# A hybrid decoder layer on one core: block stores from two queues, the block load ahead of the decay row, SiLU in the third chunk, the inverse at later places

## What is computed

```python
q, k, v = split(silu(short_conv(concat([q, k, v]), conv_w)))     # q, k then made unit length
a_mat = where(strict, (k * beta) @ k.T * decay, 0)               # per head and chunk
t_mat = triangular_solve(eye + a_mat, eye)                       # the inverse
u, w = t_mat @ (v * beta), t_mat @ (k * beta * exp(g))
v_new = u - w @ s                                                # s: the running state
o = (q * exp(g)) @ s + (q @ k.T * decay) @ v_new
s = s * exp(g_last) + k_dec.T @ v_new
y = layer_norm(alpha * x + concat([rms_norm(o) * norm_w * silu(z_a), swa * silu(z_b)]) @ w_out)
```

## Time and profile before

| | |
|---|---|
| time, median of 3 runs | 1247.62 us (1246.43 to 1248.07) |
| profiled execution: its own time | 1249.48 us |
| profiled execution: span from the first to the last instruction | 1247.7 us |
| busy: PE, PEld, DVE, ACT, POOL | 1149.6, 900.9, 650.1, 505.5, 198.0 us |
| mean granted clock of TensorE | 0.970 |

### The profile page before, as it was taken

The page is one execution under the profiler, slowest core; times in us unless marked ns, Lnnn a source line. Parts: engine busy times, 40 slices in busy tenths (PEclk is TensorE's granted clock), DMA queues, the critical chain, the costliest instruction groups (busy, mean ns, idle before and its releaser), DMA issues. The chain is left out here.

```text
span 1247.7 us, 19748 instructions
## 1 busy us (share of the span) xinstructions
PE 1149.6 (92%) x7340; PEld 900.9 (72%) x7340; DVE 650.1 (52%) x1996; ACT 505.5 (41%) x1475; POOL 198.0 (16%) x268
## 2 busy tenths in 40 slices
PE   4988989888999999999999999999899989899997
PEld 2766767666777868786786878777686868687776
DVE  3345554645355464646356364745437363636565
ACT  3363636363352625353352433336233534353220
POOL 4522323122210101023000101012100000000340
PEclk9998989898999999999999999999999999999999
DMA  6753745545572543632436362625244343522232
GB/s 212 287 191 123 252 164 161 179 136 153 161 237 102 164 160 104 211 127 78 150 132 193 124 192 79 201 84 172 85 165 157 110 137 110 168 79 61 94 109 84
DMA packets 63887, 183.57 MB, mean 147 GB/s; under 512 B 16240, under 2 KB 28976, under 8 KB 50480
## 3 DMA queue, kind: packets, MB, share of 16 engines
q1 hardware_dynamic: 63792, 182.32, 44.1%
HBM read 138.22 MB, written 44.07 MB: 146 GB/s over the span
## 5 line engine op out<-in xcount | busy, mean ns | idle before, releaser
L760 PE MATMUL bank<-xr,w 128*128 128x512 f32 x2496 | 684.8, 414 | 5.1 <-ACT conv_in L1091 3.2
L760 PEld LDWEIGHTS bank<-xr,w 128*128 128x128 f32 x2496 | 455.5, 193 | 108.5 <-issue 14.8
L733 POOL TENSOR_TENSOR x_tile<-x_tile,gain 128x256 f32<-128x256 f32 x40 | 28.1, 736 | 716.6 <-DVE x_tile L1484 716.6
L810 PE MATMUL bank<-wo,y_split 128*128 128x512 f32 x432 | 118.8, 409 | 0.0
L810 PEld LDWEIGHTS bank<-wo,y_split 128*128 128x128 f32 x432 | 76.2, 188 | 17.1 <-issue 1.9
L1410 DVE SCALAR_TENSOR_TENSOR kq<-conv_in,convw_all,kq 128x512 f32<-128x512 f32 x96 | 76.5, 796 | 3.4
L1332 ACT ACTIVATE blocks<-bank 128x128 f32<-128x128 f32 x64 | 17.8, 277 | 149.0 <-PE bank L1027 148.8
L1605 DVE TENSOR_TENSOR y_step<-blocks,y_cols 128x60 f32<-128x60 f32 (+14 forms) x240 | 49.7, 207 | 49.7 <-DMA blocks<-n_spill 42.0
L1227 ACT ACTIVATE score<-score,neg_max 128x256 f32<-128x256 f32 (+1 forms) x128 | 62.5, 490 | 16.8 <-DVE neg_max L1572 16.8
L1297 ACT ACTIVATE blocks<-bank 128x256 f32<-128x256 f32 (+1 forms) x64 | 24.4, 382 | 105.1 <-PE bank L974 73.7
L1692 DVE SCALAR_TENSOR_TENSOR t<-bank,cols_all,v_tok 128x128 f32<-128x128 f32 x64 | 22.3, 348 | 84.8 <-PE bank L1012 84.8
(11 more groups left out here) (214 smaller groups left out, 1762.1 us busy)
## 6 DMA issues: line engine op xcount, KB each, us to landing
w<-w_split SPq DMA_DIRECT2D x78, 1024.0 KB, 5.0
w_split<-w SPq DMA_DIRECT2D x26, 1024.0 KB, 4.9
blocks<-n_spill SPq DMA_DIRECT2D x16, 512.0 KB
y_spill<-y_out SPq DMA_DIRECT2D x30, 256.0 KB, 6.3
y_tile<-w_in SPq DMA_DIRECT2D x13, 512.0 KB, 6.1
x_tile<-w_in SPq DMA_DIRECT2D x13, 512.0 KB, 6.2
y_tile<-y_spill SPq DMA_DIRECT2D x12, 512.0 KB, 6.7
x_tile<-x SPq DMA_DIRECT2D x12, 512.0 KB, 5.6
```

The costliest lines, as they stand in the source:

```text
L733: nc.gpsimd.tensor_tensor(res[:, part], res[:, part], gain[:, part], ALU.mult).then_inc(scaled.sem, 1)
L760: ins = nc.tensor.matmul(bank[at % 2][:], w[:, turn % 3, wp, k, :], xr[:, xp, k], start=(step == 0), stop=(step == 3 * KT - 1))
L810: ins = nc.tensor.matmul(bank[at % 2][:], y_place(t)[:, yp, k], wo[:, k, wp, half * UNIT:(half + 1) * UNIT], start=(step == 0), stop=(step ...
```

## The change

1. `store_blocks` on SyncE's queue issues five of the eight block stores; ScalarE issues the other three, behind the squares of q and ahead of the scaled k, with a wait for `n_ready`.
2. `load_blocks` stands right behind the block stores; the decay row, the input loads of long slots, weights and the spill come behind it.
3. `AT_VTOK` goes from 0.13 to 0.16. In `Places`, `first` (the place of t0, from which the inverse's places count) goes from 0.47, 0.42, 0.36 (short, middle, long) to 0.49, 0.44, 0.375, `step0` and `step` from 0.665 and 0.082, 0.62 and 0.092, 0.6 and 0.097 to 0.685 and 0.077, 0.635 and 0.088, 0.605 and 0.096.
4. The SiLU stands ahead of the third chunk's squares where the jobs that it needs end early enough, which is so in short and middle slots, and ahead of the fourth's as before in long ones. In middle slots the job bz changes places with o1. The split of the next y tile on VectorE moves from the third to the fourth chunk.
5. The exponential of the decay row (`eg_row`) stands ahead of the squares of k.
6. Where a slot's last job is followed by a `w_hi` (slots 0 and 1), that is held until behind the block stores of the next slot.

```diff
--- before.py
+++ after.py
@@ -39,6 +39,7 @@
 BASE = 16
 HALF = P // 2
 PIECES = 4
+SP_BLOCKS = 5
 TILES_W = 26
 TAIL = 12
 
@@ -62,7 +63,7 @@
     if i == AH - 1:
         return ["z"] + (["o0", "o1"] if s > 0 else []) + unit_start
     if s == 1 or s == 2:
-        return ["q", "k", "v", "z", "o0", "o1", "bz", "bq"]
+        return ["q", "k", "v", "z", "o0", "bz", "o1", "bq"]
     return ["q", "k", "v", "bz", "z", "bq"]
 
 
@@ -154,7 +155,7 @@
 
 
 AT_KK = 0.04
-AT_SCORES0, AT_VTOK, AT_TURNS0, AT_VALUES0 = 0.09, 0.13, 0.24, 0.31
+AT_SCORES0, AT_VTOK, AT_TURNS0, AT_VALUES0 = 0.09, 0.16, 0.24, 0.31
 
 
 class Places:
@@ -163,9 +164,9 @@
     def __init__(self, n):
         fill = slot_span(n)
         short, long = fill < 160, fill > 200
-        first = 0.47 if short else 0.36 if long else 0.42
+        first = 0.49 if short else 0.375 if long else 0.44
         self.t0, self.p16, self.t16, self.p32, self.t32, self.p64, self.y12 = (first + 0.028 * a for a in range(7))
-        self.step0, self.step = (0.665, 0.082) if short else (0.6, 0.097) if long else (0.62, 0.092)
+        self.step0, self.step = (0.685, 0.077) if short else (0.605, 0.096) if long else (0.635, 0.088)
         self.scores1 = self.p16 + 0.015
         self.turns1, self.values1 = self.step0, self.step0 + 0.05
         self.base = 0.3
@@ -585,7 +586,7 @@
 
             def store_blocks(n):
                 after(sp, n_ready, n, CH)
-                for g in range(P // BASE):
+                for g in range(SP_BLOCKS):
                     part = slice(g * BASE, (g + 1) * BASE)
                     sp.dma_start(n_spill[n, g].rearrange("t a c -> a t c"), n_t[part, :, part]).then_inc(n_stored.sem, 16)
 
@@ -634,13 +635,13 @@
                     for dst, source in ((gain, ln_g), (shift, ln_b)):
                         sp.dma_start(dst[:], source).then_inc(gain_in, 16)
                 store_blocks(n)
+                load_blocks(n)
                 if i < AH - 1:
                     after(sp, pt_ready, n, 2)
                     load_decay(n + 1)
                 if i == AH - 1 and 0 < s < SBS - 1:
                     after(sp, x_low_dve, s + 1, 1)
                     load_x(s + 1, 3)
-                load_blocks(n)
                 after_jobs(n, 0.16)
                 if n > 0:
                     spill_a(n - 1)
@@ -1108,6 +1109,12 @@
                 nc.scalar.activation(own[:, EKD], own[:, EKD], ACT.Exp).then_inc(cols_ready.sem, 1)
 
             place = [0]
+            held = []
+
+            def split_weight():
+
+                while held:
+                    w_hi(held.pop())
 
             def after_job(at):
                 job = JOBS[at]
@@ -1144,7 +1151,10 @@
                 elif kind == "gT":
                     copy(g_turned, at, gt_copied)
                 if at in W_AT and W_AT[at] + 3 < TILES_W:
-                    w_hi(W_AT[at] + 3)
+                    if at + 1 < len(JOBS) and JOBS[at + 1].n > max(job.n, -1) >= 0:
+                        held.append(W_AT[at] + 3)
+                    else:
+                        w_hi(W_AT[at] + 3)
                 k = {"ba": 0, "q": 1, "k": 2, "v": 3, "kb": 4, "vb": 5, "bz": 6, "bq": 7}.get(kind)
                 if n == AH - 1 and k is not None:
                     wo_hi(k)
@@ -1242,6 +1252,9 @@
             def slot(n):
                 s, i = divmod(n, AH)
                 at = Places(n)
+                after(act, g_row_in, n, 16)
+                after(act, resid_ready, n - 1, CH)
+                nc.scalar.activation(eg_row[:], decay[:], ACT.Exp).then_inc(eg_ready.sem, 1)
                 after(act, ktok_done, n, 1)
                 for c in range(CH):
                     nc.scalar.activation(n_t[:, c], bank[4][:, c * P:(c + 1) * P], ACT.Square,
@@ -1250,9 +1263,6 @@
                 nc.scalar.activation(ln_ss[:, 0], sums_sq[:, 0], ACT.Ln, bias=eps[:, 0:1]).then_inc(ln_ready.sem, 1)
                 after(act, ln_ready, n, 1)
                 nc.scalar.activation(r_k[:], ln_ss[:, 0], ACT.Exp, scale=-0.5).then_inc(rk_ready.sem, 1)
-                after(act, g_row_in, n, 16)
-                after(act, resid_ready, n - 1, CH)
-                nc.scalar.activation(eg_row[:], decay[:], ACT.Exp).then_inc(eg_ready.sem, 1)
                 if i == 0:
                     after(act, vt_done, s, 1)
                     first = 4 * s % 8
@@ -1264,6 +1274,11 @@
                 for c in range(CH):
                     nc.scalar.activation(k_dec[:, c], bank[5][:, c * P:(c + 1) * P], ACT.Square,
                                          accum_out=sums_sq[:, 1, c:c + 1]).then_inc(sq_done.sem, 1)
+                after(act, n_ready, n, CH)
+                for g in range(SP_BLOCKS, P // BASE):
+                    part = slice(g * BASE, (g + 1) * BASE)
+                    act.dma_start(n_spill[n, g].rearrange("t a c -> a t c"), n_t[part, :, part]).then_inc(n_stored.sem, 16)
+                split_weight()
                 after(act, small, n, 3)
                 after(act, sq_done, n, 2 * CH)
                 for c in range(CH):
@@ -1314,11 +1329,16 @@
                 take(p64[high], half_tiles(bank[6])[high], 8)
                 after_jobs(n, at.y12)
                 take(y_inv[low, :, high], half_tiles(bank[7])[low], 9)
-                after_jobs(n, at.step0)
+                after_jobs(n, min(at.step0, 0.66))
                 copy_turned(n, 1)
+                silu_before = CH - 2 if silu_at(n) - n < at.chunk(CH - 2) and n < SLOTS - 1 else CH - 1
                 for c in range(CH):
+                    if c == silu_before:
+                        after_jobs(n, max(at.chunk(c), silu_at(n) - n))
+                        if c < CH - 1:
+                            silu(n, True)
                     if c == CH - 1:
-                        after_jobs(n, max(at.chunk(c), silu_at(n) - n))
+                        after_jobs(n, at.chunk(c))
                         if t is not None and i == AH - 2:
                             round_y(t + 1)
                         elif n == SLOTS - 2:
@@ -1326,7 +1346,8 @@
                         if n == SLOTS - 1:
                             round_y(14)
                             round_y(15)
-                        silu(n, True)
+                        if silu_before == c:
+                            silu(n, True)
                     after_jobs(n, at.chunk(c, 2 / 3))
                     after(act, o_done, n, c + 1)
                     nc.scalar.activation(o_scaled[:, c], bank[7][:, c * P:(c + 1) * P], ACT.Square,
@@ -1705,7 +1726,7 @@
                         convs(n, (at.p64, at.chunk(0), 1)[c])
                     if n == SLOTS - 1 and c < 3:
                         split_y(11 + c)
-                    if c == 2:
+                    if c == CH - 1:
                         if t is not None and i == AH - 2:
                             split_y(t + 1)
                         elif n == SLOTS - 2:
```

## The result

The changed kernel is slower. Its median is 1256.6 us (ten runs, 1252.5 to 1263.8) against 1247.8 us for the kernel before (ten runs, 1246.4 to 1250.8); the ratio is 1.0070, 95% interval 1.0049 to 1.0092. I had forecast 1222 us. The profiled execution of the changed kernel took 1253.1 us and is one of the low ones; its span is 1251.1 us against 1247.7, so the traces show 3.4 us of the some 9.

What follows compares the result with a forecast made beforehand. TensorE, busy 1149.6 of 1247.7 us, bounds the kernel; only its idling or low clock can be won. Savings 20.4 + 5.7 + 1.8 - 0.2 - 3.3 - 10.9 + 11.9 = 25.4 us gave 1222, range 1204 to 1243.

Steps and rivals of the forecast that it cites:

- bz ahead of o1: Middle slots: VectorE normalises last, SyncE is held until 7 us into the next slot; about 4.5 us lost.
- In slots 6 and 10 L953 at 12 covers that: The transposes, 12 us into these slots, release the block load anyway, so the held SyncE queue costs nothing there.
- A landing 2 us later in slots 5 and 9: Some 2.5 MB pass ahead of the block load; t0 waits 1.9 and 2.6 us instead of 1.0 each.
- The weights behind the held queue: A weight load behind SyncE's held output store; TensorE waiting for weights was a sign of being wrong, without a size.
- In 7 and 11 the x tile comes 1.0 too late: Behind held SyncE, the x tile is 1.0 us late for VectorE and L881 in each slot, 2.0 together.
- the transposes' place: Moved 0.03 of a slot later, 1.2 to 1.5 us; block load 0.5 later in slot 10, against 0.9 gained.
- t0, all slots: TensorE's waits for the base inverse at t0 in 16 slots fall from 44.8 to 24.4 us, saving 20.4.
- third chunk's squares, L1019: New TensorE wait behind the moved SiLU: 1.5 us in slots 2 and 12 to 14, 2.45 in 0 and 1; 10.9.
- clock, busy time saved: TensorE's low-clock losses behind waits fall from 14 to 7, at 1.7 us each; 11.9 us saved.
- The rival of the near waits: Twelve remaining TensorE waits between 1.37 and 2.4 us also lower the clock; 20.4 more, 1242 us; chance 0.20.
- the slower rival: ScalarE's DMA issues cost 1.8 us each, scaled k comes 5.5 behind N, TensorE waits at L948; 1261 us; chance 0.08.
- The earlier N: Moved SiLU and exponential bring N 1.85 us earlier in slots 13, 14, 3 and 15, 3.1 in 1 and 2.

Runs made afterwards that it cites:

- swap_back: Changed kernel with o1 ahead of bz again in the six middle slots; 1236.7 us, ratio 0.9936 to the kernel before.
- norm_early: Changed kernel, bz still ahead of o1, middle slots' output tiles normalised 0.05 of a slot behind o1's end instead of 0.1; 1237.5 us, ratio 0.9934.
- decay_first: The repaired kernel with the decay row's load ahead of the block load again; 1224.8 us, ratio 0.9822 to the kernel before.
- repaired kernel: Changed kernel with middle slots' output tiles normalised 0.05 behind o1 and the transposes at 0.13; 1223.9 us, ratio 0.9831 to the kernel before.

## Why the prediction was wrong

**The step that failed most is that of bz ahead of o1.** Its mechanism was right in each part: VectorE normalises last, SyncE is held, and the store goes out 7.1 us into the next slot, as written. Its price was not. I gave it about 4.5 us (t0 in slots 5 and 9 at 1.9 and 2.6 instead of 1.0 each, 2.0 together in slots 7 and 11) and the chip 17 (swap_back, norm_early). Four things in that step were wrong:
- *"In slots 6 and 10 L953 at 12 covers that"*: the load went at 14.6 in both. The five stores are issued by 10.7, but they have landed only at 14.6, behind the store of 0.5 MB and the weight tile of 1 MB that were held with them.
- *A landing 2 us later in slots 5 and 9*: the load's issue alone was 5 us later, 17.5 and 17.1 us into the slot instead of the 12.1 that the transposes allow.
- *The weights behind the held queue* were named in the text, and again in its last line as a way to be wrong, but had no term in the sum. They are 11.1 us in the trace, 10.6 more than before. It is not the tile right behind the held store (in slot 5 issued at 7.5 and there at 14.0) that TensorE waited for, but the next one, which stands behind the block load and so behind the landing of the block stores. TensorE spent them there, and so the t0 waits of slots 5 and 9 came out at zero, where I had forecast 4.5: the time went to another row.
- *In 7 and 11 the x tile comes 1.0 too late*: the wait came at L811, for the copy of za, behind VectorE's late `y_out`, 3.1 us in slot 7, and 6.1 together. The swap undone leaves 3.6 of it, and slots 7 and 11 together at 177.4 us (178.0 in the changed kernel, 173.8 before). So undoing the swap gives back only 0.6 of the 4 us that these two slots lose here, though in the kernel before the swap alone costs them 7.8. With the early normalising and the transposes at 0.13 they take 172.5.

**The second is the transposes' place.** I had it as what releases the load in middle slots (0.5 later) and in slot 13, and in middle slots I netted it against 0.9 us of landing from the decay row's place, of which decay_first shows 0.2 to 0.3 and nothing in the time. In middle slots of the changed kernel with a free queue the load goes at 12.1; with 0.13 it goes at 10.8. I had asked what the split could win behind the transposes, found nothing, and gone on, instead of asking what the kernel would be without the later transposes. That was 7 us in the changed kernel and 13 once the queue was free, and in slot 3, whose transposes moved from 14.5 to 16.7 us into the slot, the t0 wait rose from 3.7 to 4.6 (forecast 4.2).

**The terms of the sum** (forecast and trace, us; a term with a plus is what came on top of the kernel before):

| term | forecast | trace |
|---|---|---|
| t0, all slots | 24.4 | 29.9 |
| of it slots 0 to 3 | 11.45 | 15.2 |
| of it slots 12 to 14 | 4.2 | 5.2 |
| scaled k, L949 | 0.9 | 1.1 |
| third chunk's squares, L1019 | 10.9 | 9.7 |
| t, L969 | 6.1 | 5.3 |
| L1021 | 2.1 | 1.3 |
| L882 and the late x tile | 2.0 | 2.5 |
| clock, busy time saved | 11.9 | 8.1 |
| weights, L761 | none | +10.6 |
| za, L811 | none | +6.1 |
| L795, gate values | none | +2.6 |
| L776 behind GpSimd and L896 | none | +2.4 |

The forecast had the span 25.4 us shorter and the trace has it 3.4 longer, and these rows make up the 28.8 us between. The scaled k, the squares of the third chunk, t and L1021 came out near their terms; the weights, za, t0, the clock and L795 are what was missed.

In slots 1 and 2 the t0 waits are 3.8 and 3.7 instead of 2.1 and 2.5. In slot 2 the inverse is ready 3.5 us earlier (27.4 us into the slot instead of 30.9), but TensorE is there 2.5 us earlier too, though its place is 0.75 later: it waits 1.9 us less ahead of L948, and over the 6 us behind that wait the granted clock is 1.00 instead of 0.72. So the wait fell by 1.0 us alone, from 4.7. The working that the forecast shows has no term for the second part. The 2.6 us at L795 are one wait in slot 3, in the unit start. The later places alone bring it too (2.7 us there in their run, 0.3 in the repaired kernel with the old places), so it belongs to the places.

Two readings of the forecast are off without moving its result. It calls 0.86 us a quarter of the 6.6, which would be 1.65; slot 13's own wait is 0.86 in the trace, and the sum uses that. By its own terms the transposes of slot 13 end at 1003.4, not 1003.2.

**The rival of the near waits is out.** In the changed kernel's trace TensorE has 17 waits between 1.07 and 2.26 us from slot 0 on, and the granted clock over the 6 us behind each of them is 1.00. The two waits for the third chunk's squares in slots 0 and 1, which the sum counted as losses, are among them (2.20 and 2.26). What lost clock instead were the waits for weights in slots 5 and 9. Below are the stretches (us, busy time by engine, then PEclk, in which 1.00 is 2.4 GHz throughout and the other level is 1.2 GHz, DMA share and GB/s) behind the 4.03 us for weights in slot 5, 2.50 at L969 in slot 8, 2.29 at t0 in slot 12 and 1.32 at L1019 in slot 13:

```profile
442.50:448.50 6.00, 5.99 (x23) 4.43 (x25) 5.31 (x23) 0.54 (x1) 0.00 (x0) 0.55 1.06 365
677.80:683.80 6.00, 5.99 (x69) 4.16 (x71) 3.88 (x14) 1.70 (x6) 0.00 (x0) 1.00 0.26 61
972.00:978.00 6.00, 6.00 (x48) 3.98 (x48) 3.64 (x7) 0.98 (x2) 0.00 (x0) 0.72 0.49 175
1061.40:1067.40 6.00, 6.00 (x35) 5.24 (x36) 1.88 (x6) 3.37 (x16) 0.00 (x0) 1.00 0.31 96
```

The length of the wait alone does not tell it: the 2.50 us of slot 8 cost no clock, the 2.29 of slot 12 did.

**The block load in short slots** went out 2.4 us earlier (10.5 us into slot 13 instead of 12.9) where I had 2.2, and the price of the issues came out near its term as well. The issues in slot 13 (the three stores, then the scaled k with the idle time ahead of it):

```profile
1012.56 1.45 ACTq L1280 DMA_DIRECT2D n_spill<-n_t  x3
1014.11 1.14 ACT L1285 ACTIVATE k_dec<-bank,kd_s 128x128 f32<-128x128 f32 x4 [1.67 <-issue]
```

Three issues take 1.67 us of ScalarE, 0.56 each, against the 1.4 of the forecast and the 5.5 of the slower rival. **That rival was wrong in its mechanism**, though it had the direction, and that its 1261 us lies near the measured 1256.6 is luck: eight stores on SyncE instead change nothing in the changed kernel, and the split brings 16 us alone. The kernel was slower by another way, one that I had put inside the sum at a quarter of its size.

**The earlier N** was real: it is begun 5.1 us into slots 3, 13 and 14 instead of 6.9, and into slots 1 and 2 instead of 8.3 (forecast 1.85 and 3.1 earlier; slot 15 has 1.1). I gave it a large part of the t0 gain. But the split alone, with N as late as before, is at 0.9872. And in the repaired version with the SiLU of short slots ahead of the fourth chunk N is late again, 7.1 us into slots 13 and 14, and the time is the same (0.9838 against 0.9831). Since in short slots the load waits for the stores or for the transposes, and these wait for the scaled k, an earlier N moves the wait from L948 to t0 and L1019.

## What to carry over

When a queue waits for an operation, price every transfer behind it on that queue, and the landing of small transfers behind the big ones that are let go together, not the held time alone; a consequence that is named in a list of risks belongs in the sum with a number. When two conditions release the same transfer, an earlier one is worth nothing if the same change makes the other later: ask for each part what it would be worth without the others, and test the parts alone. Here two of the parts, the split of the stores and the later places of the inverse, carried the whole gain.

## What the runs showed of the hardware

VectorE's four 128x128 operations of the decay took 3.02 us while GpSimd scaled and shifted a tile, and 1.14 us without it (rows above). The base inverse is longer beside GpSimd too: from its first operation to the start of its last (L1612 before, L1633 after) it takes 8.7 us in slots 0 to 2, where GpSimd splits weights for 2.9 us of that time, and 6.8 in slots 12 to 14, where GpSimd stands still (both kernels).

DMAs of 4 KB that are issued behind a weight tile and two loads of x were all there only 5.1 us after the last issue had ended (slot 5 of the changed kernel: 427.16, and the block load, which waits for them, at 432.31), and 1.0 us after it where nothing stood ahead (repaired kernel with eight stores, slot 13: 999.90 and 1000.94). It is not the order on one queue alone: ScalarE's three stores in slot 5 had no transfer ahead of them on their own queue, and took 5.2 to 6.2 us from issue to landing, against 1.5 to 1.9 in slot 13.

The Trainium skill (DMA: Bandwidth & Descriptors, Issuing engines are not separate DMA queues) says that a second issuer saves issue time alone. The trace agrees on the size of the issue time (five stores take 2.39 us on SyncE, eight 3.85, rows above), and the runs show what it can be worth: 16 us over 16 slots in the kernel before, about half of it by the clock, 12 us in the repaired kernel, and nothing in the changed one.
